# Expert weights loaded as whole matrices, and one head group's keys kept ordered by residue class

## The reference

```python
for layer in range(2):
    xn = rmsnorm(h, mixer_norm[layer])
    if layer == 0: mix = retention(xn, ret_w_in, ret_w_out)
    else:
        k_sh, v_sh = shared_kv(h, kv_norm, w_kv, k_norm)
        mix = dilated_attention(xn, k_sh, v_sh, w_q, q_norm, w_o, rel_bias)
    h = h + mix
    hn = rmsnorm(h, ffn_norm[layer])
    h = h + hier_moe(hn, ...)      # top-1 of 4 groups, then top-2 of 8 experts, SwiGLU
```

## Time and profile before

| | |
|---|---|
| time, median of 3 runs | 1474.73 us (1472.74 to 1475.68) |
| profiled execution: time, span | 1475.01 us, 1473.1 us |
| PE, DVE, ACT, POOL busy | 79%, 29%, 23%, 4% of the span |
| mean granted TensorE clock | 0.908 |
| moved by DMA | 489.02 MB, mean 332 GB/s |

### The profile page before, as it was taken

One profiled execution on the slowest core, in us unless ns is written; L12 is line 12 of the kernel. 1 busy time (PEld: TensorE's weight loads), 2 busy tenths in 40 slices (PEclk: granted clock), 3 DMA queues, 4 the chain that ended last, 5 costly groups with the idle time before them and its releaser, 6 DMA issues.

```text
span 1473.1 us, 16103 instructions
## 1 busy us (share of the span) xinstructions
PE 1159.2 (79%) x6928; PEld 704.6 (48%) x6928; DVE 428.9 (29%) x793; ACT 343.8 (23%) x561; POOL 65.2 (4%) x120
## 2 busy tenths in 40 slices
PE   6999997857757677575999999997867757577575
PEld 6986785413323133131788877775413323133131
DVE  6744535100100101002866555635100100101001
ACT  4334423100001011011655464642100001001010
POOL 2000000000000000000300051020000000000000
PEclk9999998989989888898899999998988899889897
DMA  9553478999999999999555474469999999999996
GB/s 343 201 175 112 174 303 336 421 421 421 421 421 422 421 422 421 420 421 379 136 184 174 171 169 133 174 175 423 421 421 422 422 421 421 421 422 422 421 421 250
DMA packets 90553, 489.02 MB, mean 332 GB/s; under 512 B 6032, under 2 KB 6240, under 8 KB 40816
## 3 DMA queue, kind: packets, MB, share of 16 engines
q1 hardware_dynamic: 86064, 480.52, 81.0%
q0 software_dynamic: 4000, 7.36, 2.9%
q10 hardware_dynamic: 416, 0.07, 0.0%
HBM read 486.77 MB, written 1.17 MB: 331 GB/s over the span
## 4 chain that ended last, share of the span: by engine, by line
PE 60%; DMA 32%; DVE 3%; ACT 3%; issue 1%; POOL 0%; SPq 0%; ACTq 0%; DVEq 0%
DMA ring_more<-in_exp_down 13%; DMA ring<-in_exp_down 13%; PE triple L1115 8%; PE bank L1077 8%; PE triple L356 7%; PE triple L358 7%; PE triple L357 7%; DMA ring_rows<-in_exp_down 4%; PE bank L1157 4%; PE triple L1138 4%; PE bank L1138 3%; ACT work L1174 2%; PE bank L356 2%; PE bank L358 2%; PE bank L357 2%
## 5 line engine op out<-in xcount | busy, mean ns | idle before, releaser
L1115 PE MATMUL triple<-ring,work 128*32 128x512 f32 x1232 | 246.4, 679 | 105.5 <-DMA ring_more<-in_exp_up 31.1
L1115 PEld LDWEIGHTS triple<-ring,work 128*32 128x32 f32 x1232 | 67.3, 122 | 240.6 <-issue 240.6
L1233 DVE TENSOR_TENSOR work<-work,triple 128x512 f32<-128x512 f32 x16 | 11.0, 688 | 527.2 <-PE triple L1115 527.2
L1115 PE MATMUL triple<-ring_more,work 128*32 128x512 f32 x624 | 138.7, 681 | 28.8 <-DMA ring_more<-in_exp_up 17.7
L1138 PE MATMUL triple<-ring,work 128*32 128x512 f32 x304 | 86.5, 930 | 89.9 <-DMA ring<-in_exp_down 39.2
L1077 PEld LDWEIGHTS bank<-work,hn 128*128 128x128 f32 x512 | 124.4, 334 | 40.3 <-issue 36.8
L1077 PE MATMUL bank<-work,hn 128*128 128x128 f32 x512 | 130.3, 411 | 15.4 <-DVE h L1242 12.2
L1242 DVE TENSOR_TENSOR h<-h,bank 128x512 f32<-128x512 f32 x64 | 44.0, 687 | 272.7 <-PE bank L1157 272.7
L338 DVE TENSOR_TENSOR lo_b<-ring,hi_b 128x2048 fp32r<-128x2048 f32 x40 | 90.3, 2288 | 20.3 <-ACT hi_b L331 20.1
L1174 ACT ACTIVATE work<-bank,gains 128x128 f32<-128x128 f32 x128 | 36.6, 368 | 240.6 <-PE bank L1077 240.6
L338 DVE TENSOR_TENSOR ring_lo<-ring,ring_hi 128x2048 fp32r<-128x2048 f32 x32 | 72.0, 2288 | 25.1 <-ACT ring_hi L331 25.0
(11 more groups left out here) (305 smaller groups left out, 1878.4 us busy)
## 6 DMA issues: line engine op xcount, KB each, us to landing
ring<-in_exp_gate SPq DMA_DIRECT2D x40, 2048.0 KB, 32.8
ring<-in_exp_down SPq DMA_DIRECT2D x38, 2048.0 KB, 33.2
ring<-in_exp_up SPq DMA_DIRECT2D x37, 2048.0 KB, 33.1
ring_more<-in_exp_gate SPq DMA_DIRECT2D x20, 2048.0 KB, 32.9
ring_more<-in_exp_down SPq DMA_DIRECT2D x20, 2048.0 KB, 33.2
ring_more<-in_exp_up SPq DMA_DIRECT2D x19, 2048.0 KB, 33.2
ring<-in_w_kv SPq DMA_DIRECT2D x12, 2048.0 KB, 8.9
ring<-in_ret_w_in SPq DMA_DIRECT2D x11, 2048.0 KB, 8.9
```

The source lines that it names most:

```text
L1115: last = nc.tensor.matmul(bank[2 + kind][rows, :], m_x[:, k, rows], w[e][:, kk * FF:(kk + 1) * FF], start=(k == 0), stop=(k == KD - 1))
```

## The change

It has two parts. In the MoE a tile becomes one expert's whole matrix: one run of 16 KB per partition instead of two of 8 KB. Group 0's gate and the last group's down keep the old tiles (`by_halves`). `weights` waits for all four tiles of a kind before its first half, and `used` releases a tile after the second half.

In the attention group 0's k stays in the order of classes. The near scores are then in that order, so `turned` can transpose plain blocks of 128 columns, and `biased` reads the near bias with a stride of four elements (`keys_by_class`). The own and the near part are now separate instructions: the two own parts first, each with a wait for its end, then the two near parts, which take the own minimum as their start value.

```diff
+        def keys_by_class(view):
+            return view.rearrange("p (u a) -> p a u", a=CLASSES)
...
+        def by_halves(it, kind):
+            return (it, kind) in ((0, 0), (EXPERT_GROUPS - 1, 2))
...
+                if not by_halves(it, j // PER_GROUP):
+                    e = it * PER_GROUP + j % PER_GROUP
+                    sp.dma_start(slot(at).rearrange("p (e c) -> p e c", e=1),
+                                 rows[kind][:, e:e + 1, :]).then_inc(s_ring[at], 16)
+                    return
...
-                found = []
-                for pair in range(2):
-                    n = it * MOE_TILES + kind * PER_GROUP + 2 * half + pair
-                    at = slots_in_order[first + n]
-                    pe.wait_ge(s_ring[at], 16 * loads_through(first + n))
-                    found += [slot(at)[:, e * TILE // 2:(e + 1) * TILE // 2] for e in range(2)]
+                if not by_halves(it, kind):
+                    tiles = [it * MOE_TILES + kind * PER_GROUP + e for e in range(experts)]
+                    found = [slot(slots_in_order[first + n])[:, half * TILE // 2:(half + 1) * TILE // 2] for n in tiles]
+                else:
+                    tiles = [it * MOE_TILES + kind * PER_GROUP + 2 * half + pair for pair in range(2)]
+                    found = [slot(slots_in_order[first + n])[:, e * TILE // 2:(e + 1) * TILE // 2]
+                             for n in tiles for e in range(2)]
+                if half == 0 or by_halves(it, kind):
+                    for n in tiles:
+                        pe.wait_ge(s_ring[slots_in_order[first + n]], 16 * loads_through(first + n))
...
-                elif e % 2 == 1:
+                elif e % 2 == 1 if by_halves(it, kind) else half == 1:
                     last.then_inc(s_used, 1)
...
-                            near = d_p[(2 * pr + b) % 4][:, t * (W + P):t * (W + P) + S]
                             at = kt * S + t * P
-                            for side in range(2):
-                                keys = near[:, 2 * kt + side::CLASSES]
-                                last = nc.tensor.matmul(out[side * PER_CLASS:(side + 1) * PER_CLASS, at:at + P],
-                                                        keys, ident, start=True, stop=True)
+                            near = t * (W + P) + kt * P
+                            last = nc.tensor.transpose(out[:, at:at + P],
+                                                       d_p[(2 * pr + b) % 4][:, near:near + P], ident)
...
-                elif j // 2 == 0:
-                    dst = d_k[:, :, 0, :].rearrange("p i (u a) -> p i a u", a=CLASSES)[:, :, 2 * t:2 * t + 2, :]
-                    src = src.rearrange("p i (a u) -> p i a u", a=2)
...
+                def part(odd, at, width, bias, first, smallest):
+                    score = bank[SC_BANKS[odd]][:, at:at + width]
+                    p = d_p[(2 * pr + odd) % 4][:, t * W + at:t * W + at + width]
+                    if width == S:
+                        score, p = (v.rearrange("p (a u) -> p a u", a=CLASSES) for v in (score, p))
+                    return V.tensor_tensor_reduce(out=p, in0=score, in1=bias, scale=-1.0, scalar=first,
+                                                  op0=ALU.add, op1=ALU.min, accum_out=smallest)
                 for odd in range(2):
                     hd = 2 * pr + odd
                     dve.wait_ge(a_sc, 4 * pr + 2 * t + odd + 1)
-                    V.tensor_tensor_reduce(
-                        out=d_p[hd % 4][:, t * W:(t + 1) * W], in0=bank[SC_BANKS[odd]][:, 0:W],
-                        in1=d_bias(hd)[:, t * S:t * S + W], scale=-1.0, scalar=3.0e38, op0=ALU.add, op1=ALU.min,
-                        accum_out=d_min[:, pr % 2, t, odd:odd + 1]).then_inc(a_sum, 1)
+                    chain(part(odd, own, P, d_bias(hd)[:, S:S + P], 3.0e38, d_own_min[:, odd:odd + 1]))
+                for odd in range(2):
+                    hd = 2 * pr + odd
+                    part(odd, near, S, keys_by_class(d_bias(hd)[:, t * 3 * P:t * 3 * P + S]),
+                         d_own_min[:, odd:odd + 1], d_min[:, pr % 2, t, odd:odd + 1]).then_inc(a_sum, 1)
```

More of the change, by code:

```diff
@@ L1089, in weights, with used @@
                     return [slot(OVER_SLOT + kind)[:, half * TILE // 2:(half + 1) * TILE // 2]]
-                found = []
-                for pair in range(2):
-                    n = it * MOE_TILES + kind * PER_GROUP + 2 * half + pair
-                    at = slots_in_order[first + n]
-                    pe.wait_ge(s_ring[at], 16 * loads_through(first + n))
-                    found += [slot(at)[:, e * TILE // 2:(e + 1) * TILE // 2] for e in range(2)]
+                if not by_halves(it, kind):
[8 more added lines that the diff above has]
+                        pe.wait_ge(s_ring[slots_in_order[first + n]], 16 * loads_through(first + n))
                 return found
-            def used(last, e, half):
+            def used(last, e, kind, half):
                 if over:
@@ L1118, in group_pe @@
                             if kk == KD // 2 - 1:
-                                used(last, e, half)
+                                used(last, e, kind, half)
                     if kind == 0 and half == 0:
@@ L1142, in group_pe @@
                             if kk == 1 and nh == 1:
-                                used(last, e, half)
+                                used(last, e, 2, half)
                     if half == 1 and nh == 0:
@@ L1291, in build @@
         d_min = sb("row_min", [P, 2, TT, 2])
+        d_own_min = sb("own_class_min", [P, 2])
         d_den = sb("row_sum", [P, 2, TT, 2])
@@ L1818, in biased @@
                         dve.wait_ge(a_tp, 3 * (pr - 1))
+                near, own = (0, S) if t == 0 else (P, 0)
+                def part(odd, at, width, bias, first, smallest):
[5 more added lines that the diff above has]
+                                                  op0=ALU.add, op1=ALU.min, accum_out=smallest)
                 for odd in range(2):
```

## The result

The changed kernel takes 1453.37 us (median of 4 runs, 1452.91 to 1457.19) against 1473.74 us for the kernel before on the same chip (4 runs, 1471.95 to 1475.68): a ratio of 0.9863, 95% interval 0.9842 to 0.9885. It is faster by 20.4 us, where 19.6 were forecast. Its profiled execution has a span of 1451.2 us, against 1473.1.

A forecast was written before the change was run, and what follows sets the result against it. DMA was taken to bound the MoEs and PE the attention. Savings of 12.5 us from whole matrices and 7.1 from the attention, 19.6 together, took 1475.0 to 1455.4 us (median forecast 1455.2), with a range of 1449 to 1468.

The forecast's parts named there:

- Whole matrices: MoE weight loads: 16 KB runs mean fewer packets at 9.2 ns each; 170 tiles x 0.074 us save 12.5 us.
- Rivals 1 and 2: MoE loads: rate stays 421 GB/s, 1468 us, chance 0.13; or packet cost a third, 1463 us, chance 0.12.
- The waits for a whole kind: MoE: PE waiting for four tiles instead of two never lets the load queue run dry; cost 0.
- the 11 named as a sign: MoEs: PE should show pieces of 64 L1132 records with idle time of about 11 us.
- rival 4: MoEs: longer rests keep PE's clock at 1.2 GHz and PE becomes the bound; 1505 us, chance 0.03.
- cost 0 at both ends: MoE start and end: with gate and down kept in halves there, waits cost 0, or 1 us if not hidden.
- Pairs 0 to 3: Attention: PE never waits for `biased` there, so eight `turned` save 5.8 us, of which 5.5 are counted.
- 0.72 for each `turned`: Attention, PE: `turned` with b of 0 or 1 falls from 1.16 to 0.44 us, saving 0.72 each.
- Pairs 4 to 7: Attention: five `turned` save 3.6 us, less 1.2 for longer `biased` and 0.8 for a wait: gain 1.6.
- the upper bound of 0.7: Attention, VectorE: each `biased` grows by 0.4 us, at most 0.7 if the strided bias read costs.
- a wait at scores(7, 1) takes about 0.8: Late attention: `biased(7, 0)` comes late, so a PE wait takes about 0.8 of the 3.6 us saved.
- Rival 3: Attention: VectorE and the bias chain take most of the gain, 2 or 3 us stay; 1460 us, chance 0.07.

The follow-up runs named there:

- e1: The changed kernel with the attention of the kernel before, so only the MoE tiles are changed: 1460.79 us against 1474.32, ratio 0.9917.
- e3: Tiles made of quarters of four experts' matrices, 4 KB runs, with the waits of the kernel before: 1501.55 us, one run.
- e4: The changed kernel with whole matrices everywhere, also the first group's gate and the last group's down: 1470.98 us, one run.
- e5: The changed kernel with the near bias read without the stride, so attention values are wrong but the work is the same: 1455.92 us, one run.
- e8: The changed kernel without the wait between the two own parts of `biased`; each near part waits for its own part alone: 1453.15 us, one run.
- e10: e8 with the second head's bias of pairs 6 and 7 loaded by SP's queue instead of POOL's: 1454.35 us, ratio 0.9858 to the kernel before.
- e12: e8 plus four unread matmuls behind the first half of down in each MoE's last group: 1450.42 us, ratio 0.9847 to the kernel before.
- e2: The changed kernel with the MoE loads and waits of the kernel before, so only the attention is changed: 1467.57 us, ratio 0.9961.
- the relaxed one: The changed kernel's attention without the wait between the two own parts of `biased`, as in e8, which took 1453.15 us.

## Why the prediction was right, and where it was not

**Whole matrices, 12.5 us: right.** By medians e1 gives 13.5, and the mechanism, 9.2 ns for a packet, held over a third length of run (e3). (126.15 MB in 300 us is 0.4205 MB per us and not the prediction's 0.4213, so its price should have been 9.0 ns and not 9.2: 0.002 us per tile.) The streams are 7.2 and 6.6 us shorter; forecast were 82 x 0.074 = 6.1 and 88 x 0.074 = 6.5. Rivals 1 and 2 needed 421 and 423 to 424 GB/s and fall with 428.

**The waits for a whole kind, 0: right.** The rests of PE in a group of the changed kernel, timeline:

```profile
537.88 1.03 PE L1132 MATMUL triple<-ring,work 128*32 128x512 f32 x1 [8.77 <-DMA ring<-in_exp_up]
...
547.25 0.75 PE L1145 MATMUL bank<-kept,work 128*128 128x128 f32 x4 [0.95 <-DVE work L1250]
557.46 1.03 PE L1155 MATMUL triple<-ring,work 128*32 128x512 f32 x1 [9.46 <-DMA ring_more<-in_exp_down]
...
571.08 5.00 PE L1090 MATMUL bank<-work,hn 128*128 128x128 f32 x20 [0.87 <-DVE h L1259]
```

Rests are 6.2 to 9.5 us long, not the 11 named as a sign. Each starts the next piece at 1.2 GHz (1.03 to 1.08 us a matmul), and the clock comes back inside it: 0.86 on average against 0.88. PE is busy for 69% of the time, so rival 4 falls. The prediction's cost 0 at both ends holds only because of the exceptions, and it never priced what they avoid: 17.6 us by e4.

**Pairs 0 to 3, 5.5 us: 7.3.** The mis-sized term is "0.72 for each `turned`". It is the difference of two pieces of the chain, 1.16 and 0.44, and stops at the end of the block. The old block cost more behind it too. The chain of the kernel before, the first v projection matmul behind each of the two kinds of block:

```profile
862.59 0.43 PE triple L356
...
864.62 0.24 PE triple L356
```

So 0.72 + 0.19 = 0.91 us could be read ahead of time. The timeline of PE before, across one block:

```profile
861.03 0.40 PE L358 MATMUL triple<-hi_b,x_lo 128*128 128x512 f32 x1
861.36 1.23 PE L1506 MATMUL bank<-kept,ring 128*64 128x128 f32 x16
862.52 0.50 PE L356 MATMUL triple<-hi_b,x_hi 128*128 128x512 f32 x1
862.86 0.40 PE L357 MATMUL triple<-lo_b,x_hi 128*128 128x512 f32 x1
```

and in the changed kernel:

```profile
857.75 0.40 PE L358 MATMUL triple<-hi_b,x_lo 128*128 128x512 f32 x1
857.99 0.60 PE L1522 MATMUL bank<-kept,ring 128*128 128x128 f32 x4
858.35 0.47 PE L356 MATMUL triple<-hi_b,x_hi 128*128 128x512 f32 x1
858.66 0.39 PE L357 MATMUL triple<-lo_b,x_hi 128*128 128x512 f32 x1
```

From the start of L358 to the start of L357 it is 1.83 us before and 0.91 now, and 7.3 / 8 = 0.91.

**Pairs 4 to 7, a gain of 1.6: a loss of 3.0, and none at best.** Two steps failed. `biased` grew by 0.9 us and not by 0.4, over the upper bound of 0.7: 0.2 for each near part from the stride (e5), the rest the waits and the fixed time of four instructions. And the term "a wait at scores(7, 1) takes about 0.8" looked for one late event; PE waits for VectorE at four of the eight `scores`. Both `scores` of a pair use the same two PSUM banks, so the second waits for `biased` of the first, and between two `scores` stand only three to six matmuls of the output projection and, from pair 5 on, a `turned`, which is what became shorter. PE's busy time fell by 4.9 us (46.9 to 42.1, e8) and its idle time rose by 5.0 (0.8 to 5.8). Of these 5.8, 4.0 are `scores` waiting for `biased` and 1.8 are transposes waiting for the exponentials or for the copies of the blocks ahead of them out of PSUM. In e5, with `biased` at 1.55 us, they are 3.6 and 2.0, and the stretch is 47.7, as before: a shorter `biased` moved some of the wait to the transposes. The clock fell too in four of the nine traces with the new attention, another 1.3 to 1.9 us. Rival 3 described this, but with POOL's bias chain as its cause, and e10 to e12 show that this is not it. What sets the 47.7 of every version without a dip was not isolated further.

**What was not in the sum.** The end gained 2.3 us by the clock and the start 2.2. The start is scatter for the most part: it runs from 244.6 to 248.8 over the kernels with the new loads (e4 left aside), from 244.4 to 247.8 over those with the old. So the total agreed to 1 us by luck, since misses of both signs cancelled. That e2's 6.8 us meets the 7.1 forecast for the attention is luck too: 5.5 + 1.6 were forecast, and its trace has 7.3 and a loss of 2.2. Against 19.6 the span gave 1.3 more in the streams, 1.8 more in pairs 0 to 3, 4.6 less in pairs 4 to 7, 4.5 more at the start and the end, and 0.7 less ahead of pair 0: 21.9. The medians of e1 and e2, 13.5 and 6.8, are what a reader should keep.

## What to carry to other kernels

In a stage that its loads set, count packets: two rates at two lengths of run give a price per packet, and that price forecasts a third. Make runs long in the middle of such a stage and keep the pieces small at its two ends, where the first release and the work behind the last byte lie open. An engine's saving counts only where it isn't about to wait for the very engine that the change made slower; measure it from start to start, and look at the granted clock of the stretch before a wait or a queue is blamed.

## What the runs showed of the hardware

- A packet of the weight loads costs 9.0 to 9.5 ns of a DMA engine beside its bytes, alike for runs of 2, 4, 8 and 16 KB (387, 409, 421, 428 GB/s).
- The two-source reduction on VectorE takes 0.48 us for 256 columns, and 0.65 to 0.71 with a stride of four float32 in the bias or of 64 in the result. In a queue the next starts after 0.41 us without a stride, 0.51 to 0.54 with the one in the result, 0.58 to 0.62 with the one in the bias.
- A wait for the end of the instruction ahead on VectorE moves the next start from 0.21 to 0.33 us behind a part of 128 columns.
- Behind rests of 1.28, 0.45 and 1.66 us TensorE ran at 1.2 GHz for 3.4 to 6.8 us in all three profiled executions of the changed kernel's attention (it, e2 and e4). Behind 1.03, 0.2 and 1.42 us (the relaxed one) it did in one of four.
- Four matmuls without a reader in a rest of 4.5 us kept TensorE at 2.4 GHz for the work behind them; the kernel before became 0.39% faster with them, of which the two places explain 3.6 of 5.8 us.
